# Moving the weight-rounding step of the gate projections behind the exponentials in ScalarE's order

## Chip, cores and metric

The kernel runs on one core of one Trainium2 chip. The metric is the device time of one execution in microseconds (us).

## What is computed

The reference is a two-part model block on 256 tokens of width 1024. The change lies in the first part, in the sparse attention with its gates. Cut to what matters:

```
h = rmsnorm(x, norm_mix_pre)
z = h @ w_in                      # xr, gr, q, kc, vc, ..., gm_rnn, gm_attn
y_rnn  = rg_lru(...) * gelu(gr)
y_attn = nsa(q, ...)              # softmax over selected and window keys, 16 heads
y = sigmoid(gm_rnn) * y_rnn + sigmoid(gm_attn) * y_attn
x = x + rmsnorm(y @ w_out, norm_mix_post)
...                               # feed-forward, then a second block with two expert layers
```

The three projections `gr`, `gmr` (`gm_rnn`) and `gma` (`gm_attn`) are the "gates" of this document. Each is 1024 x 1024.

## The kernel before

Every engine has its own written-out order of instructions, and the engines meet at semaphores only. The stage of interest is the attention stage. `attention_order()` (L75 on) lists its work in 16 rounds, one for each unit u: unit u is a pair of heads `j = u // 2` and a half `t = u % 2` of the tokens. Round u holds, in this order: `score u`, the gate blocks n whose entry in `HALF_UNITS` is u, `turn u-2` (transposes of the probabilities) and `value u-3`. Round 1 has eight more transposes, "cmp_turn". All engines walk this same list. An even unit has 128 keys in each of its four rows of scores, an odd one 256.

`HALF_UNITS = (0, 0, 0, 1, 1, 2, 2, 3, 4, 4, 5, 6, 6, 7, 8, 8, 9, 9, 10, 11, 12, 13, 14, 15)` spreads 24 gate blocks (numbered 0 to 23, each 128 columns of weights) over the rounds: three in round 0, two in rounds 1, 2, 4, 6, 8 and 9, one in each other round.

A gate block goes through these steps:

- The weights (128 x 1024) come by DMA into one of 8 slots of `weight_ring`.
- ScalarE rounds them into `z_high`, which has four buffers (`high_part`, `start_high`, the copy at L1726). It waits until TensorE has freed the block four places earlier.
- VectorE forms the rest, `ring_low = weights - z_high` (`low_part`, `start_low`, L2243). It waits for that `z_high`.
- TensorE multiplies both parts (`split_columns`, 16 matmuls, recorded at L901), into a PSUM bank. It waits for the semaphore `z_low` that L2243 raises, and for the bank to be drained.
- ScalarE copies one half of the bank (`half_copied`, L1731), VectorE adds the other (`halves_added`, L2249), and ScalarE applies tanh or gelu in the next round (`shape_gate`, L1739 and L1742).

The weights of gate block n+2 are split in the round of gate block n. VectorE does so in its "gate" step: `low_part(NK + u + 2)`, then `halves_added` of block u. Blocks 0 to 3 are split before the stage and blocks 22 and 23 in rounds 12 and 13.

A unit goes through these steps: TensorE's `score` (four products into two banks); VectorE adds the bias (L2721, two instructions), takes the row maxima (L2345), and then does the normaliser of the unit before (L2685, L2687, L2691), on which TensorE's `turn` waits; ScalarE's four exponentials (L1694) wait for the maxima; ScalarE drains the transposes (`turn`, L1663); TensorE's `value` waits for that drain; VectorE drains the value bank (L2735). There are eight PSUM banks, given in turn to the jobs. After the last round come the output projection (`mix_rows`, partly inside rounds 16 to 18), the feed-forward part and the second block. POOL multiplies the shaped gates into the recurrence's result (L2152, L2157, L2160).

The functions that the diff touches, with their line numbers:

Of the kernel before, what the change touches and what calls it, by code (L numbers as in the profile page):

```python
# [21 lines left out]
NK = D // P  # L22
# [48 lines left out]
GATES = [("gma", 0), ("gr", 0), ("gr", 1), ("gr", 2), ("gma", 1), ("gr", 3), ("gmr", 0), ("gmr", 1), ("gma", 2), ("gmr", 2),  # L71
         ("gmr", 3), ("gma", 3)]
HALF_UNITS = (0, 0, 0, 1, 1, 2, 2, 3, 4, 4, 5, 6, 6, 7, 8, 8, 9, 9, 10, 11, 12, 13, 14, 15)
# [3 lines left out]
def attention_order():  # L77
    order = []
    for u in range(len(UNITS) + 3):
        if u < len(UNITS):  # L80
            order.append(("score", u))
        order += [("gate", n) for n, at in enumerate(HALF_UNITS) if at == u]
        order += [("mix", n) for n, at in enumerate(MIX_ROUNDS) if at == u]
        if u == 1:
            order.append(("cmp", 0))
        if 0 <= u - 2 < len(UNITS):
            order.append(("turn", u - 2))
        if 0 <= u - 3 < len(UNITS):
            order.append(("value", u - 3))
    return order  # L90
# [516 lines left out]
def build(nc, x_in, memT_in, weights, consts, where, rows_in, peer_uv, out):  # L607
# [5 lines left out]
    with ctx:  # L613
# [5 lines left out]
        def sem(name):  # L619

            if name not in named:
                named[name] = ctx.enter_context(nc.semaphore(name))
            return named[name]
# [196 lines left out]
        def bank(key):  # L820
            return ps[banks[ids[key]]]
# [831 lines left out]
        def _(act):  # L1653
# [4 lines left out]
            def drain(key, pieces):  # L1658

                wait_filled(act, key)  # L1660
                for n, (o, i, f, kw) in enumerate(pieces):
                    last = n == len(pieces) - 1
                    done(act.activation(o, i, f, **kw), "drained_by_act" if last else "act_step")  # L1663
# [25 lines left out]
            def softmax_unit(nm_sem, n, parts, exp_sem):  # L1689

                act.wait_ge(sem(nm_sem), n)
                for k, (tile, nm, total) in enumerate(parts):
                    last = k == len(parts) - 1
                    done(act.activation(tile, tile, ACT.Exp, bias=nm, accum_out=total), exp_sem if last else "act_step")  # L1694
# [21 lines left out]
            def high_part(m):  # L1716

                start_high(len(STARTS) + m, HD ** -0.5 if m < NK else 1.0)

            def start_high(i, scale=1.0):  # L1720

                slot = split_no(i)
                if i >= SPLITS:
                    act.wait_ge(sem("weight_free"), RING + split_no(i - SPLITS) + 1)
                act.wait_ge(sem(f"weights_loaded{slot % RING // PAIR}"), 16 * (slot // RING + 1))
                done(act.activation(z_high[:, i % SPLITS, :], ring[:, slot % RING, :], ACT.Copy, scale=scale), "z_high")  # L1726

            def half_copied(key, dst):

                wait_filled(act, key)  # L1730
                done(act.activation(dst, bank(key)[:, S:2 * S], ACT.Copy), "z_half")  # L1731

            def shape_gate(n):

                name, i = GATES[n // 2]
                wait_drained(act, ("att_gate", n))
                if name != "gr":
                    v = (gma if name == "gma" else gmr)[:, 2 * i + n % 2, :]
                    done(act.activation(v, v, ACT.Tanh, scale=0.5), f"{name}_shaped")  # L1739
                elif i == 3 and n % 2 == 1:  # L1740
                    v = gr.rearrange("p k s -> p (k s)")
                    done(act.activation(v, v, ACT.Gelu_apprx_tanh), "gr_shaped")  # L1742
# [70 lines left out]
            for n in range(2):  # L1813
                at = slice(HD * n, HD * n + HD)
# [24 lines left out]
            for kind, u in attention_order():  # L1839
                if kind == "score" or (kind == "turn" and u >= len(UNITS) - 2):  # L1840
                    for n in unshaped:
                        shape_gate(n)
                    unshaped = []
                if kind == "score":
                    for n, at in enumerate(HALF_UNITS):
                        if at == u and 1 < n < 2 * len(GATES) - 2:
                            high_part(NK + n + 2)
                    E = (att_E if UNITS[u][1] else att_E0)[u % 3]
                    softmax_unit("att_max", u + 1, [(E[:, n // 2, n % 2, :], pair_nm[:, u % 3, n:n + 1],
                                                     pair_sum[:, u % 3, n:n + 1]) for n in range(4)], "att_exp")  # L1850
                if kind == "gate":
                    unshaped.append(u)
                    name, i = GATES[u // 2]
                    half_copied(("att_gate", u), {"gma": gma, "gr": gr, "gmr": gmr}[name][:, 2 * i + u % 2, :])
                if kind == "cmp":
                    act.wait_ge(sem("lru_scanned"), 1)
                    for i in range(8):
                        key = ("cmp_turn", i)
                        t, q4 = i // 4, i % 4
                        drain(key, [(cmp_PT[0:NCMP, q4 * 4:q4 * 4 + 4, t * P:(t + 1) * P],  # L1860
                                     bank(key)[0:NCMP, :].rearrange("p (a s) -> p a s", a=4), ACT.Copy, {})])
                if kind == "turn":
                    for i in range(1 + UNITS[u][1]):
                        key = ("att_turn", 2 * u + i)
                        drain(key, [(att_PT[u % 2][:, 4 * i:4 * i + 4, :],
                                     bank(key)[:, :].rearrange("p (a s) -> p a s", a=4), ACT.Copy, {})])
# [202 lines left out]
            for n in range(SLOTS + 2 * LATER):  # L2069
                for name, what in ACT_STEPS.get(n, []):  # L2070
# [41 lines left out]
                    if name == "dil_q":  # L2112
                        o, u = what
                        blocks((f"dil_q_{o}_{u}", 0), dqT[:, u % 3 * 3:u % 3 * 3 + 3, :], 3)
                    if name == "dil_exp":
                        o, u = what
# [3 lines left out]
                    if name == "dil_turn":  # L2120
                        o, u = what
# [910 lines left out]
```

## Time and profile before

| | |
|---|---|
| median of 3 runs | 2081.31 us (2081.23 to 2082.42) |
| the profiled execution | 2081.23 us |
| its span | 2079.1 us |
| TensorE matmul, busy share of the span | 91% |
| VectorE, ScalarE, POOL | 67%, 43%, 29% |
| mean granted TensorE clock | 0.980 |

The span runs from the first recorded instruction to the last; 2.1 us of the execution's time lie around it. The busy shares are averages over stages that differ much, so the stage of the change is read by itself. L901 is the line of a helper that issues nearly all matmuls, so that TensorE's rows are told apart by their operands: `x_low_high,z_high` and `x_low_high,ring_low` are gate blocks; `64*128 64x128` and `64x256` with both operands in `arena` are scores; `const_tile` as the moving or standing operand means a transpose; `15*64 15x128` begins a value.

### The profile page before, as it was taken

The page shows a single profiled execution, that of the slowest core. Times are in us where ns is not written, and L with a number is a line of the kernel's source. Part 1 is how long each engine was busy: PE and PEld are TensorE (multiplying, and loading weights), DVE is VectorE, ACT ScalarE, POOL GpSimd, SP SyncE. Part 2 cuts the span into 40 slices and gives each one's busy share as a digit, 9 for nine tenths or more (in the row PEclk, how much of TensorE's full clock was granted, in tenths as well). Part 3 has the DMA queues.
Part 4 walks back from the last instruction along what each step waited for, and adds up shares of the span by engine and source line. Part 5 has one row for each costly group of instructions (what it writes and reads, how often), then busy time and mean ns, then how long its engine had stood idle before and what let it go on. Part 6 is the DMA issues. An engine that isn't in the chain of part 4 may idle for free. (4 is left out here: it accounts for less than half of the span.)

```text
span 2079.1 us, 24554 instructions
## 1 busy us (share of the span) xinstructions
PE 1888.3 (91%) x7948; PEld 1175.8 (57%) x7948; DVE 1385.1 (67%) x2957; ACT 892.6 (43%) x2409; POOL 599.1 (29%) x560
## 2 busy tenths in 40 slices
PE   8999999999998989878989989889999989778776
PEld 8888678887855645423556535546565455332222
DVE  8888576666837676899444545666865566994444
ACT  5757454454624433434324623333455334343332
POOL 0002100000014335444433333333334333444331
PEclk9999999999999999998999999999999999999999
DMA  6633455545549999999999999999999999999997
GB/s 259 224 124 104 168 205 183 191 153 197 196 158 414 421 418 400 421 421 415 421 421 422 420 422 421 416 421 421 414 412 409 422 420 415 420 413 422 422 421 302
DMA packets 99914, 714.50 MB, mean 344 GB/s; under 512 B 11088, under 2 KB 11216, under 8 KB 14416
## 3 DMA queue, kind: packets, MB, share of 16 engines
q0 software_dynamic: 76608, 549.28, 64.1%
q1 hardware_dynamic: 22752, 162.54, 20.9%
q8 instruction: 63, 1.03, 0.2%
q10 hardware_dynamic: 432, 1.16, 0.1%
q14 instruction: 59, 0.48, 0.1%
HBM read 711.89 MB, written 1.05 MB: 343 GB/s over the span
## 5 line engine op out<-in xcount | busy, mean ns | idle before, releaser
L1432 PE MATMUL bank<-arena 128*128 128x512 f32 x2048 | 978.6, 616 | 164.5 <-ACT arena L2048 163.1
L2483 DVE SCALAR_TENSOR_TENSOR arena<-arena,x_tok 128x1024 f32<-128x1024 f32 x512 | 619.0, 1225 | 463.0 <-DMA arena<-peer_uv,arena 446.9
L2202 POOL DMA_INDIRECT arena<-peer_uv,arena x512 | 567.5, 1108 | 897.8 <-PE bank L1432 771.5
L1432 PEld LDWEIGHTS bank<-arena 128*128 128x128 f32 x2048 | 375.0, 194 | 651.3 <-issue 341.5
L2041 ACT ACTIVATE arena<-arena 128x1 f32<-128x1 f32 x512 | 103.1, 201 | 860.2 <-DVE arena L2483 859.3
L901 PEld LDWEIGHTS bank<-xT,weight_ring 128*128 128x128 f32 x1504 | 199.6, 194 | 42.5 <-issue 35.9
L901 PE MATMUL bank<-xT,weight_ring 128*128 128x128 f32 (+1 forms) x1504 | 208.7, 292 | 0.8 <-DVE xT L2226 0.8
L2035 ACT ACTIVATE arena<-const_tile,arena 128x128 f32<-128x128 f32 x512 | 198.2, 387 | 0.0
L2048 ACT ACTIVATE arena<-arena 128x128 f32<-128x128 f32 x512 | 197.7, 386 | 0.5
L901 PE MATMUL bank<-x_low_high,z_high 128*128 128x512 f32 (+1 forms) x480 | 135.8, 351 | 0.0
L1177 PE MATMUL bank<-x_split,w_split 128*128 128x512 f32 x704 | 127.4, 339 | 2.6 <-DVE x_split L2763 2.6
L1177 PEld LDWEIGHTS bank<-x_split,w_split 128*128 128x128 f32 x704 | 109.2, 188 | 19.6 <-issue 2.8
L2745 DVE TENSOR_TENSOR w_split<-weight_ring,w_split 128x1024 fp32r<-128x1024 f32 x66 | 80.8, 1226 | 36.8 <-ACT w_split L1876 36.0
L901 PE MATMUL bank<-x_low_high,ring_low 128*128 128x256 f32 x368 | 104.1, 283 | 0.0
L901 PEld LDWEIGHTS bank<-x_low_high,z_high 128*128 128x128 f32 x480 | 83.8, 190 | 15.0 <-issue 2.9
L847 POOL DMA_DIRECT2D row_ring<-rows_in x10 | 5.8, 586 | 287.2 <-DVEq L2299 198.7
L1876 ACT ACTIVATE w_split<-weight_ring 128x1024 fp32r<-128x1024 f32 x66 | 69.8, 1061 | 42.7 <-PE bank L1177 26.6
L1663 ACT ACTIVATE arena<-bank 128x512 f32<-128x512 f32 (+6 forms) x143 | 68.0, 499 | 46.0 <-PE bank L901 38.5
L901 PE MATMUL bank<-arena 128*64 128x128 f32 (+10 forms) x664 | 73.0, 305 | 1.7 <-DVE arena L2249 1.0
L901 PEld LDWEIGHTS bank<-x_low_high,ring_low 128*128 128x128 f32 x368 | 70.8, 192 | 0.0
L901 PEld LDWEIGHTS bank<-arena 64*128 64x128 f32 (+6 forms) x664 | 52.6, 161 | 27.0 <-issue 23.3
L901 PE MATMUL bank<-weight_ring,arena 128*128 128x512 f32 (+1 forms) x192 | 64.9, 528 | 0.2 <-ACT arena L1663 0.2
(316 smaller groups left out, 1938.2 us busy)
## 6 DMA issues: line engine op xcount, KB each, us to landing
weight_ring<-weights SPq DMA_DIRECT2D x153, 1024.0 KB
arena<-peer_uv,arena POOLq DMA_INDIRECT x512
row_ring<-rows_in POOLq DMA_DIRECT2D x10, 512.0 KB, 5.3
arena<-weights POOLq DMA_DIRECT2D x5, 512.0 KB, 7.9
const_tile<-consts POOLq DMA_DIRECT2D x1, 1849.0 KB, 9.5
x_tok<-x_in SPq DMA_DIRECT2D x2, 512.0 KB, 4.5
memT<-memT_in POOLq DMA_DIRECT2D x1, 1024.0 KB, 6.2
const_tile<-weights POOLq DMA_DIRECT2D x1, 1024.0 KB, 5.1
```

Source lines behind the costliest of these rows:

```text
L847: e.dma_start(rows[:, n % NROW, :], rows_in[n:n + 1, :].to_broadcast([P, D]))\
L901: ins = pe.matmul(o, lhsT, rhs, start=start, stop=stop, is_transpose=turn or None)
L1177: ins = pe.matmul(o, lhsT, rhs, start=start, stop=stop)
L1432: ins = pe.matmul(b[:, :], diag[n % DIAGS], gbuf[n % GBUF][:, 1, h * 512:(h + 1) * 512], start=n % P == 0, stop=n % P == P - 1)
L1663: done(act.activation(o, i, f, **kw), "drained_by_act" if last else "act_step")
L1876: done(act.activation(w_split[n % SPLITS][:, 0, :], ring[:, slot % RING, :], ACT.Copy), "slot_high")
L2035: done(act.activation(gate_diag[n % 2], ident, ACT.Copy, scale=w[:, s:s + 1]), "gate_diag")
L2041: done(act.activation(hdot[:, s:s + 1], hdot[:, s:s + 1], ACT.Gelu), "peer_gelu")
L2048: done(act.activation(diag[n % DIAGS], gate_diag[n % 2], ACT.Copy, scale=hdot[:, s:s + 1]), "diag_ready")
L2202: pool.indirect_dma_start(gbuf[n % GBUF].rearrange("p a d -> p (a d)"), None, peer_uv, bass.IndirectOffsetOnAxis(ap=expert[t][:, s:s + 1]. ...
L2483: dve.scalar_tensor_tensor(u, u, 1.0, x[:, t, :], ALU.mult, ALU.mult, accum_out=hdot[:, s:s + 1])\
L2745: done(dve.tensor_tensor(w[:, 1, :], ring[:, slot % RING, :], w[:, 0, :], ALU.subtract), name)
```

## The change

ScalarE's order within a round is altered, nothing else. Before, ScalarE rounded the weights of all the blocks n+2 that belong to round u (those with 1 < n < 22) ahead of the exponentials of unit u. After, it rounds the weights of block n+2 in the "gate" step of block n, behind the exponentials of the round and just ahead of the half copy of block n. The twenty copies are the same twenty, with the same waits.

```
@@ -1842,14 +1842,13 @@
                         shape_gate(n)
                     unshaped = []
                 if kind == "score":
-                    for n, at in enumerate(HALF_UNITS):
-                        if at == u and 1 < n < 2 * len(GATES) - 2:
-                            high_part(NK + n + 2)
                     E = (att_E if UNITS[u][1] else att_E0)[u % 3]
                     softmax_unit("att_max", u + 1, [(E[:, n // 2, n % 2, :], pair_nm[:, u % 3, n:n + 1],
                                                      pair_sum[:, u % 3, n:n + 1]) for n in range(4)], "att_exp")
                 if kind == "gate":
                     unshaped.append(u)
+                    if 1 < u < 2 * len(GATES) - 2:
+                        high_part(NK + u + 2)
                     name, i = GATES[u // 2]
                     half_copied(("att_gate", u), {"gma": gma, "gr": gr, "gmr": gmr}[name][:, 2 * i + u % 2, :])
                 if kind == "cmp":
```

In the "gate" step `u` is the number of the gate block; in the "score" step it is the unit.

## Rows read from the trace of the kernel before

**Rows 1.** The page: busy time, and the 40 slices of 52 us each.

```profile
PE 1888.3 (91%) x7948; PEld 1175.8 (57%) x7948; DVE 1385.1 (67%) x2957; ACT 892.6 (43%) x2409; POOL 599.1 (29%) x560
...
DMA  6633455545549999999999999999999999999997
```

**Rows 2.** Windows: us, busy time (instructions) by engine, granted clock, DMA share, GB/s.

```profile
120.65:233.01 112.36, 112.36 (x826) 92.02 (x824) 94.99 (x165) 79.09 (x217) 21.22 (x27) 0.99 0.32 113
121.00:124.00 3.00, 3.00 (x12) 2.52 (x12) 2.69 (x10) 0.40 (x1) 0.00 (x0) 0.61 0.00 0
250.00:300.00 50.00, 46.91 (x203) 33.28 (x202) 29.47 (x55) 25.70 (x54) 0.86 (x1) 1.00 0.58 200
```

**Rows 3.** Timeline of TensorE: start, us, line, operation, operands, count, idle before.

```profile
116.12 4.60 PE L901 MATMUL bank<-arena 64*128 64x15 f32 x72 [0.97 <-DVE arena L2249]
...
137.25 3.65 PE L901 MATMUL bank<-const_tile,arena 128*15 128x128 f32 x32
...
185.50 0.39 PE L901 MATMUL bank<-x_low_high,z_high 128*128 128x512 f32 x1
...
225.73 2.52 PE L901 MATMUL bank<-arena 15*64 15x128 f32 x28
...
278.70 8.56 PE L1177 MATMUL bank<-x_split,w_split 128*128 128x512 f32 x48 [2.63 <-DVE x_split L2763]
```

**Rows 4.** Timeline of ScalarE in the attention stage.

```profile
127.51 0.40 ACT L1694 ACTIVATE memT<-memT,arena 128x128 f32<-128x128 f32 x1 [1.24 <-DVE arena L2345]
...
134.25 0.51 ACT L1694 ACTIVATE memT<-memT,arena 128x256 f32<-128x256 f32 x1 [0.46 <-DVE arena L2345]
...
137.94 3.93 ACT L1663 ACTIVATE arena<-bank 15x512 f32<-15x512 f32 x8
...
154.78 2.00 ACT L1726 ACTIVATE z_high<-weight_ring 128x1024 fp32r<-128x1024 f32 x2
...
156.68 0.40 ACT L1694 ACTIVATE memT<-memT,arena 128x128 f32<-128x128 f32 x1
...
158.22 0.37 ACT L1731 ACTIVATE arena<-bank 128x256 f32<-128x256 f32 x1
...
181.16 0.51 ACT L1694 ACTIVATE memT<-memT,arena 128x256 f32<-128x256 f32 x1
...
183.15 0.36 ACT L1731 ACTIVATE arena<-bank 128x256 f32<-128x256 f32 x1
...
183.41 1.06 ACT L1663 ACTIVATE arena<-bank 128x512 f32<-128x512 f32 x2
```

**Rows 5.** Timeline of VectorE in the attention stage.

```profile
117.60 1.22 DVE L2243 TENSOR_TENSOR ring_low<-weight_ring,z_high 128x1024 fp32r<-128x1024 f32 x1 [1.59 <-ACT z_high L1726]
...
141.62 0.75 DVE L2721 SCALAR_TENSOR_TENSOR arena<-const_tile,bank 128x256 f32<-128x256 f32 x2 [3.10 <-PE bank L901]
...
168.45 0.28 DVE L2735 SCALAR_TENSOR_TENSOR arena<-arena,bank 128x128 f32<-128x128 f32 x1
...
168.65 0.75 DVE L2721 SCALAR_TENSOR_TENSOR memT<-const_tile,bank 128x256 f32<-128x256 f32 x2
...
169.50 0.69 DVE L2345 TENSOR_REDUCE arena<-memT 128x4 f32<-128x512 f32 x1
...
181.47 1.64 DVE L2243 TENSOR_TENSOR ring_low<-weight_ring,z_high 128x1024 fp32r<-128x1024 f32 x1
...
191.87 1.27 DVE L2721 SCALAR_TENSOR_TENSOR memT<-const_tile,bank 128x512 f32<-128x512 f32 x2
...
193.24 1.22 DVE L2345 TENSOR_REDUCE arena<-memT 128x4 f32<-128x1024 f32 x1
...
214.75 1.22 DVE L2243 TENSOR_TENSOR ring_low<-weight_ring,z_high 128x1024 fp32r<-128x1024 f32 x1
...
215.89 0.41 DVE L2249 TENSOR_TENSOR arena<-arena,bank 128x256 f32<-128x256 f32 x1
```

**Rows 6.** Timeline of POOL, the first work after the gelu.

```profile
178.75 7.04 POOL L2152 TENSOR_TENSOR arena<-arena 128x256 f32<-128x256 f32 x8 [166.62 <-ACT arena L1742]
```

More of the change, by code:

```diff
@@ L1844, in _ @@
                 if kind == "score":
-                    for n, at in enumerate(HALF_UNITS):
-                        if at == u and 1 < n < 2 * len(GATES) - 2:
-                            high_part(NK + n + 2)
                     E = (att_E if UNITS[u][1] else att_E0)[u % 3]
@@ L1852, in _ @@
                     unshaped.append(u)
+                    if 1 < u < 2 * len(GATES) - 2:
+                        high_part(NK + u + 2)
                     name, i = GATES[u // 2]
```

## The prediction

> **What bounds the kernel now.** I read the page first, for the shares [rows 1]: TensorE is busy 91% of the span, no other engine is near it, and the DMA engines, at three to six tenths through the first third, are near their full share only in the second part. That the change can matter at all depends on its own stage, so I took windows [rows 2]. From 120.65 to 233.01 us, rounds 0 to 15, TensorE is busy for 112.36 of 112.36 us. VectorE is busy for 95.0 (85%), ScalarE for 79.1, the DMA share is 0.32. Then the timelines of the three engines [rows 3 to 5], to see who waits for whom. TensorE has one idle time here, 0.97 us at 116.12, ahead of the first score. Everything else in the stage waits for TensorE: VectorE 3.10 us at 141.62, and ScalarE between its half copies. So in this stage TensorE sets the time and the other two run in its shadow. A gain inside it has nothing to take; what can be lost is the shadow. Behind the stage TensorE goes on nearly without a break (46.91 of 50 us busy, clock 1.00 [rows 2]), at a DMA share of 0.58, and its longest wait, 2.63 us at 278.70 [rows 3], is for VectorE work that hangs on TensorE's own products. Nothing absorbs a delay there, and the DMA-bound second part starts from the routing of its first expert head, which hangs on all this. I count a delay of TensorE in this stage one for one in the total.
>
> **The change, part by part.** It adds and removes no instruction. Twenty rounding copies of 1.05 us, at 0.95 us from start to start (154.78 to 156.68 [rows 4]), leave their place ahead of the exponentials and stand behind them. What was parallel becomes serial. Before, the copies lay where ScalarE waits for the maxima of unit u, so VectorE found `z_high` ready when it came to `low_part`, as at 214.75 [rows 5]. After, VectorE can begin `low_part` only when the maxima are out, the exponentials done and the copy made. Behind that wait VectorE's order holds `halves_added`, the value bank, and the scores and maxima of the next unit, for which the next exponentials wait. So the two engines form one closed loop per round, with the normaliser of the unit before alone beside ScalarE's part.
>
> The price of a loop, exponential start to exponential start:
> - four exponentials of an odd unit 1.99 us (181.16 to 183.15), of an even unit 1.54 (156.68 to 158.22) [rows 4];
> - the copy and the step to VectorE 1.08: 1.05, and about 0.03 of signal, since `low_part` starts at 117.60 after a copy that I take to end just before it [rows 5];
> - `low_part` 1.14 to the next start (214.75 to 215.89), `halves_added` 0.33 (0.41, less an overlap of 0.08), the value 0.20 (168.45 to 168.65);
> - scores and maxima of a following even unit 0.85 and 0.72 (168.65, 169.50), of a following odd one 1.37 and 1.25 (191.87, 193.24) [rows 5].
>
> An odd round with one block: 1.99 + 1.08 + 1.14 + 0.33 + 0.20 + 0.85 + 0.72 = 6.31 us. An even one: 1.54 + 1.08 + 1.14 + 0.33 + 0.20 + 1.37 + 1.25 = 6.91. A second block adds a `low_part` and a `halves_added`, 1.48 (its copy, at 0.95 + 0.26, is ready in time): 8.39 for an even round, 7.79 for round 9.
>
> How it begins. Round 0 is hardly touched: the exponentials start at 127.51 in either order [rows 4], and the one copy behind them makes VectorE about 0.5 us late. In round 1 the exponentials start at 134.76 instead of 134.25; then come copy, half copy, copy, half copy, and the eight "cmp_turn" drains start at 139.2 instead of 137.94. VectorE drains gate block 4 at 134.76 + 1.99 + 1.08 + 1.14 + 0.34 + 1.15 + 0.41 = 140.9. The eighth "cmp_turn" needs that bank, and TensorE would reach it at 137.25 + 7 x 0.45 = 140.4 [rows 3]: the first stall, about 0.5 us. The 3.10 us of idle VectorE at 141.62 take up the rest of the delay. Rounds 2 and 3 follow TensorE again, 0.55 us late; at the end of round 3 VectorE is behind, and the exponentials of round 4 start at 158.4 instead of 156.68.
>
> From there I carry the loop on: round 5 at 158.44 + 8.39 = 166.83, round 6 at 173.14, round 7 at 181.53. In round 7 ScalarE has the gelu with its two table loads between, and comes free only about 182.4. Then `low_part` of block 15 is done at 182.4 + 1.99 + 1.08 + 1.22 = 186.7, and it falls into POOL's first burst of 7.04 us [rows 6]: in such a burst the same instruction took 1.64 us instead of 1.22 (at 181.47 [rows 5]), so 187.1. TensorE wants block 15 at 185.50 + 0.55 = 186.05: a second stall, 1.1 us. Rounds 8 to 13 follow at 182.4 + 6.31 + 0.42 = 189.13, then + 8.39, + 7.79, + 6.91, + 6.31, + 6.91 = 225.44. TensorE's value of unit 11 needs the transposes of that unit drained, behind the exponentials, a copy and a half copy: 225.44 + 1.99 + 0.95 + 0.26 + 1.06 + 0.05 = 229.75. Before, it started at 225.73 [rows 3]. TensorE is then 4.0 us late, having lost it in four places: "cmp_turn" of round 1, block 15 of round 7, block 18 of round 9, and the value of unit 11. Rounds 14 and 15 have no copies; by the same sums their drains come out about even with TensorE, so I leave the delay at 4.0, with this as a risk upwards. The profiled execution took 2081.23, within 0.1 of the median: 2081.23 + 4.0 = 2085.2 us.
>
> The bounds. Ten loops are carried on; an error of 0.1 us in each (hops that the trace before doesn't show, because no engine waited there) is 1 us either way. Below: if TensorE's stall at block 15 and the delay at the value fell out for slack that I don't see, the first stall of 0.5 would remain. Above: POOL's further bursts may meet `low_part` in up to four more rounds, 4 x 0.42 = 1.7. Starting the exponentials of even rounds earlier, the only thing the change brings forward, I cost at nothing: their normaliser is hidden by VectorE's own order, and TensorE isn't waiting for it.
>
> The rows show that POOL's work stretches `low_part` by 0.42 us [rows 5, 6], and the sum above uses that. The Trainium skill ("SBUF — State Buffer", "SBUF: two separate sides") says that a VectorE instruction with two inputs in SBUF and a GpSimd instruction that reads SBUF take one port pair in turn, each for its whole length. The trace agrees in kind: only the form with both inputs in SBUF is stretched. By that rule a `low_part` could wait for the rest of a POOL multiplication, 0.88 us (7.04 by 8), instead of 0.42, and the sum would be 4.5.
>
> **The rivals.**
> - *Hidden after all: 2081.3 to 2082.* The copies run two blocks ahead of their use, and VectorE is only 85% busy. If the loop is no longer than TensorE's round, TensorE notices nothing beyond 0.5 us. For it: the slack of 17 us in VectorE [rows 2]. Against it: from the exponentials of round 4 (156.68) to those of round 13, which must start 4.31 us before the value of unit 11 (225.73), there is room for 64.7 us [rows 3, 4], and the loops with their two detours add up to 67.0, from a start that is already 1.8 late.
> - *The clock falls too: 2087 to 2089.* At 116.12 TensorE idled 0.97 us and then ran 72 small products; behind them the granted clock was at its lower level, 1.2 GHz (mean 0.61 at 121 to 124 [rows 2]), a loss of 3 x 0.39 = 1.2 us. If stalls of 1 us do that here, one to three falls add 1.2 to 3.6 us. Against it: around 2.63 us of idle time at 278.70 the clock stayed at 1.00 [rows 2, 3], so that stalls between dense gate blocks seem too weak.
> - *Faster: 2080.3 at best.* Exponentials ahead of two copies start up to 1.9 us sooner, and with them the normaliser and TensorE's transposes. It decides from the point at which TensorE waits for a normaliser; but TensorE is busy all 112.36 us [rows 2], and its one idle time at the stage's start, 0.97 us, is the most that I can name as a price. That is under the bound of 0.2%.
>
> **How the numbers follow.** My forecast, the loop that costs 3 to 6 us, gets 0.60; hidden 0.18; the clock as well 0.18; faster 0.04, nearly all of it too small to tell. About 0.2% of the time, 4.2 us, is what a measurement of this kernel can tell from no change, and my forecast lies at it: a bit over half of its chance (0.33) and the clock's 0.18 are slower, the rest of it and the hidden case are the same. Faster 0.02, same 0.47, slower 0.51. The range from 2082.0 to 2088.5 leaves out the hidden case's lower half, the far end of the clock's, and the faster one: 2 in 10. The likeliest case's own range is 2084.0 to 2087.0.
>
> **What the profile after would show.** If I am right: the exponentials of round 0 at the same time; VectorE idle before L2243 in nearly every round until ScalarE L1726, 1 to 2 us each; ScalarE idle before L1694 until L2345; TensorE with stalls of 0.5 to 1.5 us released by L2249, L2243 and L1663; the value of unit 11 near 229.8 and the shift constant from there to the end. It would be wrong if VectorE's `low_part` were already late before the change, if the loop's hops were longer than 0.03 us, or if a later stage had slack of its own.

## The result: 0.5% slower, three times what was forecast

| | before | after |
|---|---|---|
| median of 5 runs, us | 2082.26 (2081.23 to 2083.09) | 2093.42 (2090.51 to 2095.51) |
| ratio, 95% interval | | 1.0053 (1.0043 to 1.0064) |
| span of the profiled execution, us | 2079.1 | 2091.2 |

The forecast was 2085.2 us with a range up to 2088.5. The direction was right, the size was not. Two later comparisons of the same two kernels on other occasions gave 1.0041 (1.0027 to 1.0054) and 1.0037 (1.0024 to 1.0050), so 8 to 11 us in all.

The page of the changed kernel, against [rows 1]: TensorE has the same 7948 matmuls and is busy 5.6 us longer (its products ran longer, at a lower clock in places); the rest of the 12 us of span is idle time. The whole change lies ahead of the part in which the DMA share is at nine tenths.

```profile
PE 1893.9 (91%) x7948; PEld 1177.6 (56%) x7948; DVE 1381.2 (66%) x2957; ACT 891.9 (43%) x2409; POOL 607.1 (29%) x560
...
DMA  6632455554648999999999999999999999999997
```

Windows of the changed kernel (columns as in [rows 2]): the attention stage, and the start of the feed-forward part. TensorE, which was busy for all of this stage before, is idle for 4.6 us of it, and the clock's mean is 0.97.

```profile
123.06:242.18 119.12, 114.55 (x825) 93.07 (x824) 91.59 (x165) 77.61 (x213) 20.07 (x27) 0.97 0.31 107
...
259.00:310.00 51.00, 47.88 (x205) 33.83 (x200) 29.02 (x53) 24.29 (x51) 0.86 (x1) 0.97 0.52 185
```

TensorE's timeline of the changed kernel, with all its waits from the first score to the projection; it answers to [rows 3]. The first row came at 116.12 before: this execution was 2.36 us late ahead of anything that the change touches, which is to be taken off all its times when they are compared with those of before.

```profile
118.48 4.65 PE L901 MATMUL bank<-arena 64*128 64x15 f32 x72 [0.97 <-DVE arena L2248]
...
143.34 0.61 PE L901 MATMUL bank<-const_tile,arena 128*15 128x128 f32 x4 [0.50 <-DVE arena L2248]
...
189.89 0.47 PE L901 MATMUL bank<-x_low_high,z_high 128*128 128x512 f32 x1 [1.19 <-issue]
...
204.73 0.47 PE L901 MATMUL bank<-x_low_high,z_high 128*128 128x512 f32 x1 [0.58 <-issue]
...
219.94 2.52 PE L901 MATMUL bank<-arena 15*64 15x128 f32 x28 [0.36 <-DVE arena L2248]
...
233.32 3.33 PE L901 MATMUL bank<-arena 15*64 15x128 f32 x28 [1.94 <-DVE arena L2248]
...
236.57 0.79 PE L901 MATMUL bank<-x_low_high,z_high 128*128 128x512 f32 x1
...
241.23 1.02 PE L901 MATMUL bank<-arena 15*64 15x128 f32 x12
...
244.86 1.10 PE L901 MATMUL bank<-weight_ring,arena 128*128 128x512 f32 x2 [0.69 <-ACT arena L1663]
```

There are six new stalls: the eighth "cmp_turn" (0.50), block 15 (1.19), block 18 (0.58), the value of unit 9 (0.36), the value of unit 11 (1.94), and in the projection behind round 15 the first product of the third `mix_out` job (0.69). The row at 219.94 holds the 20 products of the value of unit 9 and, behind them, the scores of unit 13; its wait is ahead of the value, whose PSUM bank gate block 19 held until VectorE had drained it (L2248). The expectations below call this place the scores of unit 12. Two of the stalls have "issue" as releaser; they end where VectorE's `ring_low` is ready, which is what the matmul's `z_low` wait asks for.

VectorE's timeline of the changed kernel in an odd round (3) and at the start of an even one (4), and ScalarE's at four sets of exponentials (units 4, 5, 13 and 15) and at the last drain:

```profile
157.82 1.23 DVE L2242 TENSOR_TENSOR ring_low<-weight_ring,z_high 128x1024 fp32r<-128x1024 f32 x1 [2.10 <-ACT z_high L1726]
158.96 0.41 DVE L2248 TENSOR_TENSOR arena<-arena,bank 128x256 f32<-128x256 f32 x1
159.29 0.28 DVE L2734 SCALAR_TENSOR_TENSOR arena<-arena,bank 128x128 f32<-128x128 f32 x1
159.49 0.74 DVE L2720 SCALAR_TENSOR_TENSOR memT<-const_tile,bank 128x256 f32<-128x256 f32 x2
160.34 0.69 DVE L2344 TENSOR_REDUCE arena<-memT 128x4 f32<-128x512 f32 x1
...
163.83 1.23 DVE L2242 TENSOR_TENSOR ring_low<-weight_ring,z_high 128x1024 fp32r<-128x1024 f32 x1 [1.13 <-ACT z_high L1726]
```

```profile
161.12 0.40 ACT L1694 ACTIVATE memT<-memT,arena 128x128 f32<-128x128 f32 x1 [2.17 <-DVE arena L2344]
...
169.60 0.51 ACT L1694 ACTIVATE arena<-arena 128x256 f32<-128x256 f32 x1 [2.30 <-DVE arena L2344]
...
228.49 0.51 ACT L1694 ACTIVATE memT<-memT,arena 128x256 f32<-128x256 f32 x1 [2.30 <-DVE arena L2344]
...
241.41 0.51 ACT L1694 ACTIVATE memT<-memT,arena 128x256 f32<-128x256 f32 x1 [3.56 <-DVE arena L2344]
...
243.65 1.06 ACT L1663 ACTIVATE arena<-bank 128x512 f32<-128x512 f32 x2
```

The reader is to see a ring: VectorE idle until the copy (L1726), ScalarE idle until the maxima (L2344), in turn. The wait view adds it up (in all, times, longest): VectorE waited for `z_high` 14 times in this stage, once in each round from 0 to 13, and in none of these rounds in the kernel before.

```profile
DVE ring_low L2242 <- ACT z_high L1726: 20.4, 14, 2.1
```

Of the 12.1 us between the two spans, 2.4 are the late start, 7.7 the stage (the product after the last value starts at 259.28 instead of 249.22, less 2.36), and 2.0 come behind it: the next long wait is 3.12 instead of 2.63 us, and the 64 products behind it took 13.06 us instead of 11.34, at a mean clock of 0.97.

### The profile page after: what moved, and what is told of

Read it like the earlier page. It is cut to its first block and busy times, and to the rows that moved or that the text cites. A ratio compares the mean times of both kernels' runs of the same rounds, so it can differ in the third digit from the quotient of the medians.

```text
span 2091.2 us, 24557 instructions
## 1 busy us (share of the span) xinstructions
PE 1893.9 (91%) x7948; PEld 1177.6 (56%) x7948; DVE 1381.2 (66%) x2957; ACT 891.9 (43%) x2409; POOL 607.1 (29%) x560
## 5 line engine op out<-in xcount | busy, mean ns | idle before, releaser
L2201 POOL DMA_INDIRECT arena<-peer_uv,arena x512 | 576.6, 1126 | 888.8 <-PE bank L1432 757.8
L1663 ACT ACTIVATE arena<-bank 128x512 f32<-128x512 f32 (+6 forms) x143 | 67.8, 498 | 49.3 <-PE bank L901 41.7
L2242 DVE TENSOR_TENSOR ring_low<-weight_ring,z_high 128x1024 fp32r<-128x1024 f32 x42 | 50.9, 1223 | 26.3 <-ACT z_high L1726 25.3
```

Of the source, the lines that this page charges most:

```text
L2201: pool.indirect_dma_start(gbuf[n % GBUF].rearrange("p a d -> p (a d)"), None, peer_uv, bass.IndirectOffsetOnAxis(ap=expert[t][:, s:s + 1]. ...
L2242: ins = dve.tensor_tensor(ring_low_r[:, slot % RING, :], w, high, ALU.subtract)
```

## The experiments

Stall times below are TensorE's, from each kernel's profile; "stage" is the time from the first score to the product after the last value, 133.1 us in the kernel before. In four of the profiles (even rounds, round 13, all but 13, three bare stalls) TensorE waited 1.5 to 1.7 us ahead of the first score, not 0.97, and the clock stayed at 1.2 GHz until 124.1 to 129.5 us, not 123.4. TensorE was 1.2 to 3.2 us late from that alone. The kernel with the bare stalls, in which nothing is moved, is one of the four. This lateness is taken off wherever "late" is told below.

**1. Both kernels once more.**

> The kernel before, profiled a second time. In the first pair of profiles TensorE was already 2.36 us later at its first attention score in the changed kernel (118.48 against 116.12 us), ahead of anything the change touches, through a longer wait of ScalarE for the weight ring (4.2 us in two waits against 1.9 in one). Theory A, chance: this second profile of the unchanged kernel puts that score anywhere from 116 to 119 us, and the span moves with it. Theory B, the changed program shifts its own start: the score is again at 116.1 and only the changed kernel is late.

> The changed kernel, profiled a second time. Loop theory: from the first score (118.48 in the first profile) to the value of unit 11 (233.32) it takes 114.8 us again, within 0.3, against 109.6 in the kernel before, with the same stalls at the eighth cmp_turn, block 15, block 18, the second score bank of unit 12 and the value of unit 11. Chance theory: these stalls differ from execution to execution. Of the clock: if the falls behind the value of unit 11 and at the start of the feed-forward part, some 1.7 us each, come from the stalls, they are there again; if they are chance, one or both are missing.

The kernel before: span 2079.8, first score at 116.05, stage 133.1, no stall. The changed kernel: first score at 116.12, span 2091.2. So the late start of 2.4 us belongs to neither; it came by chance in the first profile of the changed kernel and did not in the second. The stalls came back at cmp_turn (0.48), block 15 (1.78), the value of unit 11 (1.51) and the projection (2.27); those at block 18 and at the value of unit 9 did not. The clock's fall behind block 15 had already made TensorE 1.5 us later, so that it had no need to wait there. The fourth profile (experiment 8) has the same stall at block 15 without a fall: both small stalls are there, and TensorE comes to the value of unit 11 just as late. That value came 5.8 us late instead of 5.2, and the stage took 142.8 us, 9.7 more than before. The clock fell inside the stage in two places, and at different ones: behind block 15's stall and behind the one in the projection. My "within 0.3" was too narrow. A fall at the start of the feed-forward part appeared in the unchanged kernel too (12.90 us for the 64 products); it is no mark of the change.

**2. The copies behind the exponentials, but one block further ahead.**

```
-                    if 1 < u < 2 * len(GATES) - 2:
-                        high_part(NK + u + 2)
+                    if 0 < u < 2 * len(GATES) - 3:
+                        high_part(NK + u + 3)
```

> The copies stay behind the exponentials, as in the changed kernel, but ScalarE rounds the weights of block n+3, not n+2, in the step of block n, so that VectorE finds z_high ready when it comes to low_part of block n+2. Loop theory (VectorE waits for the copy of its own round): VectorE has no wait before L2242, TensorE has none of the five stalls, and the time is that of the kernel before, 0.999 to 1.001 of it. Rival, the copies delay ScalarE's half copies and drains: the position of the twenty copies on ScalarE is the same, so the time stays at 1.003 to 1.005 of before.

2082.91 us, ratio 0.9999 (0.9990 to 1.0007). The windows of its profile show TensorE busy without a gap again, 112.00 of 112.00 us, and VectorE has no wait before L2242:

```profile
123.00:235.00 112.00, 112.00 (x822) 91.72 (x824) 94.98 (x165) 77.56 (x215) 20.95 (x27) 0.99 0.33 113
```

Nineteen of the twenty copies keep their place in ScalarE's order of the changed kernel; only which block each is for has moved on by one. The twentieth goes from round 13 to round 0. That alone is not the gain: with the copy of round 13 out of the way and the others for their own round (experiment 6) the kernel is still slower. Here the whole loss is gone. So it is VectorE's wait for a copy of its own round that costs, not the place of the copies on ScalarE.

**3. Even rounds only, odd rounds only.** `moved(r)` tells in which rounds the new order holds; in the others the copies stay ahead of the exponentials.

```
+                    for n, at in enumerate(HALF_UNITS):
+                        if at == u and 1 < n < 2 * len(GATES) - 2 and not moved(u):
+                            high_part(NK + n + 2)
...
-                    if 1 < u < 2 * len(GATES) - 2:
+                    if 1 < u < 2 * len(GATES) - 2 and moved(HALF_UNITS[u]):
                         high_part(NK + u + 2)
```

> Only the copies of even rounds (0, 2, 4, 6, 8, 10, 12) stand behind the exponentials, those of odd rounds ahead of them as before. Loop theory: an even round costs 8.4 us (two blocks) or 6.9 (one), an odd one, whose low_part no longer waits, about 4.4, so that a pair takes 12.8 against TensorE's 14.2, and 11.3 against 11.4 in rounds 10 to 13: nearly all hidden, 0 to 1 us slower than before. Rival, each moved copy costs its share by itself: 12 of the 20 copies moved cost 12/20 of 11 us, 6 to 7 us.

> The complement of the even-rounds kernel: only the copies of odd rounds (1, 3, 5, 7, 9, 11, 13) stand behind the exponentials. Loop theory: an odd round costs 6.3 us, an even one 7.4 with two blocks and 5.95 with one, so a pair takes 13.7 against TensorE's 14.2; in rounds 10 to 13 it takes 12.3 against 11.4, from the slack of rounds 8 and 9. What is left are the stall of 0.5 us in round 1 and 0.4 at block 15: 0.5 to 1.5 us slower than before. Together with the even-rounds kernel (1.6 us) that is far below the 11 us of both at once. Rival, cost by share: 8 of 20 copies, 4 to 5 us.

Even rounds (11 copies, not the 12 of the expectation): 1.0008 (0.9999 to 1.0016), no stall in the stage. Odd rounds (9 copies, not 8): 1.0020 (1.0010 to 1.0029), more than I expected. The two small stalls that I had named did not come; its one stall of any size, 2.28 us, is in the projection behind round 15, where I had none. The two intervals just overlap, but the profiles differ plainly, and the smaller half of the copies has the stall. So the price is not by share; but a place was missing in my account.

**4. Rounds 0 to 9, and rounds 10 to 13.** The same edit, with `r < 10` and `r >= 10`.

> The new order in rounds 0 to 9 (16 of the 20 copies), the old one in rounds 10 to 13. Loop theory: TensorE keeps the stalls of round 1, block 15 and block 18, 2.8 us in the changed kernel, and loses those of unit 12's scores, of the value of unit 11 and of the projection behind it: 2.8 us slower than before, up to 4.5 if the clock falls behind a stall. Rival, cost by share: 16/20 of 11, about 9 us.

> The new order in rounds 10 to 13 alone (4 of the 20 copies). Loop theory: four loops of 6.6 us against TensorE's 5.7, but from exponentials that are still on time (201.3 us), so that bank and transposes for the value of unit 11 come at 226.1 where TensorE is there at 225.7: 0.4 us slower than before, 0 to 1. With the first-ten kernel that makes about 3, not the 5 to 6 us lost up to this value with both: a delay counts only once the slack is gone. Rival: all the loss of the last rounds (2.4 us, and what the clock adds) hangs on these four copies alone, 3 to 6 us.

First ten: 1.0011 (1.0001 to 1.0021), 2.4 us by the medians, stalls 0.49 and 1.79; as expected, though the stall at block 18 was not there (the clock had fallen behind block 15). Last four: 1.0022 (1.0014 to 1.0031), 4.4 us where I expected 0 to 1. The value of unit 11 waited 0.70 us, where the sum had 0.4, and then the projection waited again:

```profile
PE bank L901 <- ACT arena L1663: 2.3, 1, 2.3
PE bank L901 <- DVE arena L2255: 0.7, 1, 0.7
```

Four copies of twenty cost as much as the rival said, for a reason that neither theory had named.

**5. Half copies ahead of the rounding copies, on both engines.**

```
                     half_copied(("att_gate", u), ...)
+                    if 1 < u < 2 * len(GATES) - 2:
+                        high_part(NK + u + 2)
...
                     halves_added(("att_gate", u), NK + u, ...)
+                    if 1 < u < 2 * len(GATES) - 2:
+                        low_part(NK + u + 2)
```

(the two `high_part` and `low_part` calls ahead of them are taken out)

> As in the changed kernel, but in each gate step ScalarE makes the half copy ahead of the rounding copy, and VectorE adds the halves ahead of low_part. The loop is as long (6.25 and 8.4 us for 6.31 and 8.39), but the bank of a gate block is free about 1.1 us sooner. If TensorE's waits that the trace puts down to L2248 (round 1, unit 12's scores, value of unit 11) are waits for the gate block's bank, the first two vanish and the third shrinks by 0.5 us to where the drained transposes bind, so 1 to 1.5 us less than the changed kernel. If the banks don't matter, the time is that of the changed kernel.

1.0041 (1.0029 to 1.0054): no less than the changed kernel. The stalls that end with L2248 did what the bank theory says: cmp_turn 0.17, none at the value of unit 9, and the value of unit 11 waited 0.81 us, for the drained transposes (L1663) instead of the gate block's bank. Block 15, which waits for `ring_low`, kept its stall (1.62). But the stall in the projection was 2.50 us, the clock fell behind it, and the two took the gain back. So the banks decide these three places, and something else decides the end.

**6. Round 13 alone, and all rounds but 13.** The third `mix_out` job takes PSUM bank 7, which the second half of unit 13's transposes filled. ScalarE drains those in round 15, behind the exponentials of unit 15.

> One copy of the twenty is moved behind the exponentials: that of round 13. My theory now: the step that the prediction missed is the PSUM bank of the third mix_out job. It is bank 7, last filled with the second half of unit 13's transposes, which ScalarE drains only behind the exponentials of unit 15; in the kernel before that drain ends at 234.6 us and TensorE is there at 235.0, so there is 0.4 us of slack. One loop in round 13 makes the exponentials of rounds 14 and 15 1.8 us late: a stall of 1.4 to 1.5 us in the projection behind round 15 and nowhere else, 1.5 us slower than before, and about 3 if the clock falls behind it. By share it would be 0.5 us.

> Nineteen copies moved, that of round 13 left ahead of the exponentials. Same theory: the stalls up to unit 12's scores stay; that at the value of unit 11 falls from 1.5 to 1.9 us to 0.5, the exponentials of rounds 14 and 15 come 1.9 us sooner and the stall in the projection falls below 1 us. 2 to 3 us less than the changed kernel. By share it would be 0.5 us less.

Round 13 alone: the stall is where I said and nowhere else, but it is 0.99 us, and the time is 1.0000 (0.9992 to 1.0009), not to be told from before. The exponentials of unit 14 came 1.9 us late and those of unit 15 only 1.2, since round 14, which has no copy, took 6.6 us instead of 7.2. All but 13: 1.0032 (1.0021 to 1.0043), by the medians 2.7 us less than the changed kernel beside it, though the intervals overlap. The value of unit 11 waited 0.46 us, as expected, but the projection still 2.23, where I had less than 1. What I had wrong: the exponentials of unit 15 came 1.5 us sooner than in the second profile of the changed kernel, but TensorE, with less to wait at the value of unit 11, also stood at the job 1.5 us sooner. The gain was in the end of the stage, not in this stall.

**7. Three bare stalls in the kernel before.** Nothing is moved; TensorE waits for one `z_low` too many ahead of blocks 6, 9 and 12.

```
+                if m - NK in (6, 9, 12):
+                    pe.wait_ge(sem("z_low"), len(STARTS) + m + 2)
                 b = begin(key)
```

> The kernel before with nothing moved; TensorE alone waits, ahead of gate blocks 6, 9 and 12, until the ring_low of the next block is there too, which in the trace of the kernel before is 1.7 to 1.8 us after TensorE gets to them. Three bare stalls between dense gate blocks, of the size of those in the changed kernel. If a stall costs its length and no more: 5.3 us slower than before. If the granted clock falls behind each, as it did behind five stalls of 1.5 us or more in the profiles so far, about 1.5 us come on top of each: 8 to 10 us, and the gate block behind the stall takes 4.5 us instead of 3.1.

2092.48 us, ratio 1.0034 (1.0020 to 1.0047). Its profile has the three stalls, and the clock at its lower level (mean 0.50, 1.2 GHz) behind each; the three blocks took 4.58, 4.54 and 4.58 us instead of 3.1. The window of the first:

```profile
149.38 0.47 PE L901 MATMUL bank<-x_low_high,z_high 128*128 128x512 f32 x1 [1.79 <-DVE ring_low L2245]
...
165.81 0.48 PE L901 MATMUL bank<-x_low_high,z_high 128*128 128x512 f32 x1 [1.88 <-DVE ring_low L2245]
...
183.65 0.47 PE L901 MATMUL bank<-x_low_high,z_high 128*128 128x512 f32 x1 [1.87 <-DVE ring_low L2245]
```

```profile
149.90:153.30 3.40, 3.40 (x12) 2.90 (x11) 0.69 (x1) 0.00 (x0) 0.00 (x0) 0.50 0.00 0
153.50:156.00 2.50, 2.50 (x18) 1.87 (x18) 0.89 (x2) 1.93 (x3) 0.00 (x0) 1.00 0.00 0
```

5.54 us of stall and 4.5 us of slower blocks make 10.0 in the profile, whose execution was the slowest of the six. The ratio of the runs, 4 to 10 us, holds both the 5.3 us of bare stalls and the 8 to 10 with a fall behind each, so it is the profile that decides, and in other executions the falls may be fewer.

**8. The last round rearranged, in the changed kernel.**

```
 ScalarE:
+                    if u == len(UNITS) - 1:
+                        turned_unit(u - 2)        # drains att_turn of unit 13
                     E = (att_E if UNITS[u][1] else att_E0)[u % 3]
                     softmax_unit("att_max", u + 1, ...
 VectorE:
-                    if u == len(UNITS) - 1:
-                        normaliser(u)
...
                     add_recurrence(u)
+                    if u == len(UNITS) - 4:
+                        normaliser(len(UNITS) - 1)
```

> The changed kernel with its last round rearranged: ScalarE drains the transposes of unit 13 ahead of the exponentials of unit 15, and VectorE does the normaliser of unit 15 behind the value of unit 12, so that banks 7 and 0, which the third and fourth mix_out jobs need, no longer wait for those exponentials. If the delay of TensorE at the end of the stage is the lateness of the exponentials of unit 15 (7.7 and 8.3 us late in two profiles, stage 7.7 and 9.7 us late), the stall in the projection (0.7 to 2.3 us) goes, with the clock's fall behind it, and the stage is 5.3 to 6 us late, as at the value of unit 11: 2 to 4 us less than the changed kernel. If instead the stall only moves on to the next wait in the projection, the time stays within 1 us of the changed kernel.

> The changed kernel beside the two, on the same chip: 1.004 to 1.006 of before, with the stall in the projection behind round 15.

> The changed kernel a third time, on the same chip as the other three and timed against the kernel before there. 1.004 to 1.006 of before. Stalls of TensorE at the same five or six places; whether the clock falls behind a given one of them may differ.

Rearranged: 1.0028 (1.0017 to 1.0038), against 1.0037 (1.0024 to 1.0050) for the changed kernel beside it: less, but the intervals overlap. The profile is plain: no wait in the projection at all; all the stalls ahead of it are the same (0.48, 1.76, 0.58, 0.36, 1.93). The gain is 1 us, not 2 to 4: the stage is 7.3 us late, not 5.3 to 6. The clock had fallen behind the 1.93 us stall, and from the value of unit 11 to that of unit 12 TensorE took 7.9 us instead of 6.3:

```profile
234.16 3.83 PE L901 MATMUL bank<-arena 15*64 15x128 f32 x28 [1.93 <-DVE arena L2254]
...
242.06 1.02 PE L901 MATMUL bank<-arena 15*64 15x128 f32 x12
```

In the first profile of the changed kernel the same slow stretch (233.32 to 241.23, 7.9 us) lies beside the lateness of the exponentials of unit 15, and only 0.69 us of waiting is left. Where the clock doesn't fall there, as in the second and third profiles of the changed kernel, TensorE arrives sooner and waits 2.27 us. The two are covered by each other, and taking one away uncovers the other.

The third profile of the changed kernel had stalls of 0.53, 1.77, 1.47 and 2.27, the fourth 0.50, 1.77, 0.54, 0.32, 1.93 and 0.70. Its stage was 9.7 us late in the third and 8.3 in the fourth.

The control to this experiment, the same last round in the kernel before, has no time: its edit leaves out ScalarE's drain of the transposes of unit 13 instead of moving it, so TensorE would wait for ever. Whether the rearrangement saves time by itself is not shown.

## Why the prediction was too small

**Where TensorE is the bound, only the shadow can be lost: right.** The stage went from no idle time to 4.6 us, and a delay in it passed to the end one for one: in the four profiles of the changed kernel another 1.2 to 2.4 us of the difference from the span of 2079.1 us come behind the stage, so nothing was given back.

**The closed loop: right; its prices a little short.** Starts of the exponentials, forecast and measured in the first profile (2.36 us taken off): round 4, 158.4 and 158.8; round 7, 182.4 and 183.1; round 9, 197.5 and 197.9; round 11, 212.2 and 212.8; round 13, 225.4 and 226.1. The odd round at 161.12 took 6.4 us from 154.70 (priced 6.31), the even one from 161.12 to 169.60 8.48 (priced 8.39). Each of these steps was 0.04 to 0.11 us short. At round 13 the exponentials were 0.7 us later than forecast, although the forecast's 0.42 us for POOL's stretch did not come in this profile. In the other three they were 1.3 later, with a stretch of 0.6. So the prices were 1.1 us short over ten rounds in all four, about what the prediction allowed for. That this loop is the cause is shown by experiment 2, which opens it and leaves nearly all else.

**The first four places of stall: right, one size by luck.** At cmp_turn 0.5 was forecast and 0.48 to 0.53 measured. At block 15 the 1.19 us of the first profile are near the forecast's 1.1 only because two errors cancel, a loop that was later and a stretch that did not come; the other three profiles have 1.77 or 1.78. Block 18 was named without a size; it had 0.58 and 0.54, and nothing where the clock had fallen behind block 15. The value of unit 9 (0.36) was not foreseen. At the value of unit 11 I let TensorE wait for the drained transposes. It waited for the bank of gate block 21, which VectorE drains 0.4 us later (releaser L2248). Together: TensorE 5.2 us late there in the first profile and 5.8 in others, not 4.0.

**The failed step: "by the same sums their drains come out about even with TensorE, so I leave the delay at 4.0".** I compared the drain of unit 13's transposes with the value that reads them and not with the next job in their bank. The third `mix_out` job needs bank 7 some 9.1 us after the value of unit 11 starts. In the kernel before, ScalarE drained that bank until 234.64 us, behind the exponentials of unit 15, and TensorE's first product into it started at 234.84:

```profile
231.34 0.51 ACT L1694 ACTIVATE memT<-memT,arena 128x256 f32<-128x256 f32 x1 [3.86 <-DVE arena L2345]
...
233.58 1.06 ACT L1663 ACTIVATE arena<-bank 128x512 f32<-128x512 f32 x2
```

```profile
234.84 1.05 PE L901 MATMUL bank<-weight_ring,arena 128*128 128x512 f32 x2
```

With a stall there, that product starts 0.15 us behind the drain's end (244.71 and 244.86 in the first profile), so there were 0.05 us of slack, less than the 0.4 of the expectation in experiment 6. The prediction has no price for round 14; it took 6.6 us in the changed kernel. By the prediction's own prices the exponentials of unit 15 would then have started at 225.44 + 6.31 + 6.6 = 238.35, which is 7.0 us after 231.34, and TensorE would have been 7.0 us late and not 4.0. Measured: 241.41 less 2.36 is 239.05, 7.7 us late, and TensorE at the job 7.7. Rounds 14 and 15 have no copies, but they do not make up for the 8.4 us by which the exponentials of unit 14 are late. In all nine profiles with a stall at this job, TensorE is there as late as the exponentials of unit 15 are, less 0.05 us: 7.7 and three times 8.2 or 8.3 in the changed kernel, 6.7 with all but round 13, 6.6 with the half copies ahead, 3.2 with the last four rounds, 2.8 with the odd rounds, 1.2 with round 13 alone. Experiments 3, 4 and 6 thus showed that this wait appears as soon as odd or late rounds are touched, and experiment 8 that it goes when the drain is moved ahead of those exponentials. The chain of waits runs over the exponentials of all rounds from 4 to 15.

**The clock: a rival that I gave 0.18, and that came true beside the main case.** I held a wait of 2.63 us at 278.70 with the clock at 1.00 behind it against it; that was one execution, and in the next one the clock fell at the same place. In the eleven profiles with such stalls, the clock fell behind 13 of 21 stalls of 1.4 to 2.5 us inside the stage, and behind none of those of 1.2 us and less. (The 0.97 us ahead of the first score, with its small products behind, are another case [rows 2].) Experiment 7 shows the cause (stalls alone bring it) and the price, 1.5 us for a gate block. How much of it reaches the end depends on what lies beside: nothing behind block 15, where the loop was the bound and later stalls shrank by as much; 1.4 us behind the stall in the projection (9.7 us of lateness at the end of the stage instead of 8.3 in the second profile).

**The sum, corrected.** The forecast's 4.0 and 3.0 more up to the exponentials of unit 15 make 7.0. The prices of the loop add 1.1. The first profile had no stretch at block 15, 0.4 less than forecast, which gives 7.7; the others had 0.2 more, which gives 8.3. The stage was 7.7 and, in the fourth profile, 8.3 us late. The clock adds 1.4 us in the stage of the second and third profile, and 1.7 to 2.7 at the start of the feed-forward part, where it fell in one of two executions of the kernel before too (1.6). With all this the profiles, less their late starts, are 9.5 to 12.1 us longer than the first one of the kernel before, and the medians of the runs 8 to 11.

**POOL beside `low_part`.** The instruction at block 15, forecast at 1.64 us, took 1.23 in the first profile and 1.82 or 1.83 in the other three, depending on how it met POOL's multiplications. By the Trainium skill ("SBUF — State Buffer", "SBUF: two separate sides") a VectorE instruction with two inputs in SBUF and a GpSimd instruction that reads SBUF have to take turns, and the one that comes second waits for the whole of the first. The traces agree: the stretch was 0, 0.4 and 0.6 us, and never longer than a POOL multiplication alone, which takes 0.74. The 0.88 of the prediction is a mean over eight of them, two of which were themselves stretched, to 1.17 and 1.72 us.

The faster rival had nothing for it: no profile shows a stall of TensorE in the stage that ends with a normaliser. The hidden case is what the kernel of experiment 2 does.

No version was faster than the kernel before. The one of experiment 2 equals it.

## What to carry to other kernels

When two engines hand work to and fro, moving an instruction of one behind its other wait can close a ring; add up the ring once round and compare it with the bound engine's period, since a copy made one block earlier costs the same and leaves the ring open. When the ring is longer, follow its lateness to the last job that hangs on it, and for each late drain ask not only who reads the data but who gets the buffer next. Here half of the moved work cost nothing that the runs can tell, and the last fifth of it about half of the loss, so a test of one part says little about the whole.

## What the runs showed of the hardware

A wait of TensorE of 1.8 us between gate blocks, with dense products on both sides, was enough for the granted clock to go from 2.4 to 1.2 GHz within 1.2 us behind it; 16 products then took 4.6 us instead of 3.1. It happened behind 13 of 21 waits of 1.4 to 2.5 us, so the same kernel gives different sums from one execution to the next. The runs of one kernel spread over 5 us and more. Three things add to that in the profiles: these falls; a first score that came at 118.3 to 118.8 us instead of 116.1 in six of the sixteen profiles (in neither of the two of the kernel before); and a clock that, at the start of the attention stage, stayed low for longer in four of them, at a price of up to 3.2 us.
